# Two-layer diffusion backbone with a PEER expert layer, fp32: latent halves ahead of the context tokens in layer one, a pace of gathers worked out per run, and layer two's modulation moved into the context tokens' merge

## What is computed

```python
for l in range(DEPTH):
    mod_l = silu(c) @ w_mod + b_mod          # 6 x 1024, the same for all latent tokens
    mod_c = silu(c_ctx) @ w_mod + b_mod      # 6 x 1024, for all context tokens
    hl, hc = modulated rms_norm of xl, xc
    a_l = neighbourhood_attention(q_l, k_l, v_l, k_ctx, v_ctx, rpb)
    m_l = latent attention of xl over the keys of ctx and xl
    s_l = spatial_gating(...)
    xl_new = xl + mod_l[2] * branch_merge(a_l, s_l, m_l, ...)
    if not last:                              # context's own attention, merge: layer one alone
        xc = xc + mod_c[2] * branch_merge(a_c, s_c, m_c, ...)
    xl_new = xl_new + mod_l[5] * peer_ffn(h2, ...)
    if not last:
        xc = xc + mod_c[5] * peer_ffn(h2c, ...)
# peer_ffn: idx = the 16 best experts per head and token
#           act = gelu(sum(exp_u[idx] * h)); out = sum(gate * act * exp_v[idx])
```

## Time and profile before

| what | value |
|---|---|
| median of 3 runs | 5605.33 us (5599.78 to 5616.61) |
| profiled execution | 5615.22 us, span of its core 5613.4 us |
| TensorE busy | 4447.6 us (79%), mean granted clock 0.867 |
| VectorE busy | 3051.5 us (54%) |
| GpSimd busy | 2763.0 us (49%) |
| ScalarE busy | 1241.3 us (22%) |
| DMA | 1651.73 MB, 294 GB/s over the span |
| of it, gathers (software queue) | 1342.34 MB |

### The profile page before, as it was taken

How to read it: one execution, slowest core, us unless ns; L and a number is a source line. 1 busy time by engine, 2 the same in 40 slices (tenths; PEclk the granted TensorE clock), 3 DMA queues, 4 the chain that set the end, 5 groups by cost and what they waited for, 6 DMA issues and landing times.

```text
span 5613.4 us, 57357 instructions
## 1 busy us (share of the span) xinstructions
PE 4447.6 (79%) x19168; PEld 2455.9 (44%) x19168; DVE 3051.5 (54%) x8176; ACT 1241.3 (22%) x3643; POOL 2763.0 (49%) x2566
## 2 busy tenths in 40 slices
PE   7989798889997887997855558999788889655555
PEld 4467643433585344653411115558533455311111
DVE  0211767776217776556676542431677655777643
ACT  1321222333212321112211112540133211111111
POOL 0000466666304655666677770000366466777776
PEclk9889898888998888998977888999888999877778
DMA  5544799988747878999999992114688799999999
GB/s 189 189 153 142 282 367 340 335 311 331 253 137 279 324 286 304 379 398 358 356 390 369 394 389 83 55 39 154 221 310 318 278 366 399 391 391 391 362 403 353
DMA packets 464130, 1651.73 MB, mean 294 GB/s; under 512 B 51168, under 2 KB 57440, under 8 KB 463840
## 3 DMA queue, kind: packets, MB, share of 16 engines
q0 software_dynamic: 368640, 1342.34, 63.2%
q1 hardware_dynamic: 95200, 305.73, 15.2%
HBM read 1645.77 MB, written 2.10 MB: 294 GB/s over the span
## 4 chain that ended last, share of the span: by engine, by line
PE 50%; POOL 15%; DVE 13%; DMA 11%; issue 7%; ACT 3%; SPq 0%; DVEq 0%; POOLq 0%; ACTq 0%; PEldq 0%
PE banks L647 16%; PE banks L925 10%; DMA vb<-in_peer_v_dram,idx 8%; POOL vb L1446 8%; POOL ub L1435 7%; DVE ub L1386 5%; PE banks L736 4%; PE banks L663 3%; PE banks L773 3%; PE banks L835 3%; PE banks L812 2%; PE banks L758 2%; PE banks L823 1%; DMA ub<-in_peer_u_dram,idx 1%; PE banks L715 1%
## 5 line engine op out<-in xcount | busy, mean ns | idle before, releaser
L1435 POOL DMA_INDIRECT ub<-in_peer_u_dram,idx x1280 | 1424.1, 1113 | 2270.7 <-DVE idx L1374 1375.1
L925 PE MATMUL banks<-vb,dg 128*64 128x512 f32 x5120 | 1571.7, 741 | 695.7 <-DMA vb<-in_peer_v_dram,idx 626.4
L1386 DVE CUSTOM_DVE_ANT_0 ub<-ub,h2cur 128x1024 f32<-128x1024 f32 x1280 | 1529.6, 1223 | 611.1 <-DMA ub<-in_peer_u_dram,idx 485.9
L1446 POOL DMA_INDIRECT vb<-in_peer_v_dram,idx x1280 | 1338.3, 1046 | 561.0 <-issue 342.5
L925 PEld LDWEIGHTS banks<-vb,dg 128*64 128x64 f32 x5120 | 406.7, 160 | 1596.1 <-issue 1336.4
L647 PE MATMUL banks<-region,wring 128*128 128x256 f32 x3840 | 882.2, 390 | 35.8 <-ACT region L989 25.3
L647 PEld LDWEIGHTS banks<-region,wring 128*128 128x128 f32 x3840 | 738.7, 195 | 215.8 <-issue 104.9
L1135 ACT ACTIVATE dg<-consts,wgt 128x64 f32<-128x64 f32 x1280 | 358.4, 337 | 836.5 <-PE banks L925 425.3
L647 PE MATMUL banks<-h2T,wring 128*128 128x256 f32 x1280 | 316.9, 406 | 21.1 <-ACT h2T L989 21.1
L1329 DVE SCALAR_TENSOR_TENSOR region<-region,banks 128x256 f32<-128x256 f32 x120 | 50.5, 421 | 486.0 <-PE banks L647 485.9
L736 PE MATMUL banks<-region,wring 128*128 128x256 f32 (+1 forms) x1056 | 260.7, 404 | 48.0 <-ACT region L989 48.0
(11 more groups left out here) (146 smaller groups left out, 4004.9 us busy)
## 6 DMA issues: line engine op xcount, KB each, us to landing
wring<-w_gate_dram SPq DMA_DIRECT2D x120, 512.0 KB, 5.0
wring<-w_mod_dram SPq DMA_DIRECT2D x96, 512.0 KB, 4.6
wring<-w_pq_dram SPq DMA_DIRECT2D x80, 512.0 KB, 5.4
wring<-w_branch_dram SPq DMA_DIRECT2D x60, 512.0 KB, 3.6
wring<-w_out_dram SPq DMA_DIRECT2D x40, 512.0 KB, 4.7
ub<-in_peer_u_dram,idx POOLq DMA_INDIRECT x1280, 6.6
vb<-in_peer_v_dram,idx POOLq DMA_INDIRECT x1280, 6.6
region<-in_na_rpb_dram SPq DMA_DIRECT2D x64, 256.0 KB, 3.0
```

The source lines that it names most:

```text
L925: ins = nc.tensor.matmul(bank(ACC[a])[64 * g:64 * g + 64, :], dg[:, n % DG_RING, :], vb[:, n % V_RING, a * 512:(a + 1) * 512], start=first ...
L1386: nc.vector.tensor_tensor_reduce(out=ub[:, n % U_RING, :], in0=ub[:, n % U_RING, :], in1=h2cur[:, g, :], scale=1.0, scalar=0.0, op0=ALU.mu ...
L1435: pool.indirect_dma_start(ub[:, n % U_RING, :], None, u_rows, bass.IndirectOffsetOnAxis(ap=idx[:, u % IDX_RING, j:j + 1], axis=0)).then_in ...
L1446: pool.indirect_dma_start(vb[:, n % V_RING, :], None, v_rows, bass.IndirectOffsetOnAxis(ap=idx[:, u % IDX_RING, j:j + 1], axis=0)).then_in ...
```

## The change

1. **Order.** Layer one now computes context's keys and values (`"kc"`, without queries), then half A and half B's `kq_stage`, `na_stage` of both, and the rest of A and of B. Only then come context's own stages: `kq_stage` again, with queries (keys and values are computed a second time), attention, merge, query. `TILES` is reordered to A, B, context. Layer two begins with A and B, and takes context's keys last.
2. **Pace.** `schedule` is run twice. The first time it notes the cost at marks; between the third projection of one `query_stage` and that of the next lies one run. The second time each run gets its own cost per background step, so that some 120 steps fit: 4.3 within `query_stage`, and outside it 3.47 (half B, both layers), 4.04 to 4.84 (context) and 1.29 to 4.84 (layer two's `kq_stage`). By the numbers that the code computes, in order: 4.3, 3.4715, 4.3, 4.0435, 4.3, 1.2892, 4.3, 4.8393, 4.3, 3.4715.
3. **Modulation.** `modrow` has one buffer per layer, the first in `vb`, the second in `region`; `cS` and `cT` have tiles of their own (the index ring gives 22 to 21 for it). `modr` writes 2 rows of each group of 32, so ScalarE copies four pieces of 2x256 and not one of 128x256; and a chunk's `modt` stands ahead of the next chunk's `modr`. Layer two's 24 chunks are computed in context's `merge_stage`.

Counted from the list that each kernel builds (steps that have their dot products or their sums there):

| place | steps before (dots/sums) | after |
|---|---|---|
| layer one, ahead of the first query stage | 0 | 0 |
| layer one, first query stage | 13/2 (context) | 13/2 (half A) |
| B: mla, merge with the norm behind it, query (each layer) | 40, 46, 16 | 47, 56, 17 |
| layer one: kq A, kq B, na, mla A, merge A, query A | 18, 15, 41, 37, 4/15, 13/2 | none |
| context, layer one: kq, na, mla, merge with the norm, query | none | 18, 10, 18, 58, 16 |
| layer two: kq of context, kq A, kq B | 11, 17, 0 | 0, 57, 50 |
| forced, in layer two's start | 13, then 100/111 | 24/35 |
| layer two: na, mla A, merge A | 0 | 0 |
| forced, at the end | 141/152 | 123/134 |

The diff, cut to its core:

```diff
-U_RING, V_RING, IDX_RING, DG_RING = 6, 6, 22, 8
+U_RING, V_RING, IDX_RING, DG_RING = 6, 6, 21, 8
-BG_STEP = 4.2
+RUN, QUERY_STEP = 120, 4.3
...
-        TILES = [(0, 0), (0, 1), (0, 2), (0, 3), (0, 4), (0, 5), (1, 2), (1, 3), (1, 4), (1, 5)]
+        TILES = [(0, 2), (0, 3), (0, 4), (0, 5), (0, 0), (0, 1), (1, 2), (1, 3), (1, 4), (1, 5)]
...
         def emit(step, cost=0.0):
             plan.append(step)
-            owed[0] += cost
-            while owed[0] >= BG_STEP:
-                owed[0] -= BG_STEP
+            pace["cost"] += cost
+            if pace["steps"] is None or not pace["marks"]:
+                return
+            step_cost = pace["steps"][len(pace["marks"]) - 1]
+            pace["owed"] += cost
+            while pace["owed"] >= step_cost:
+                pace["owed"] -= step_cost
                 if not bg_step():
-                    owed[0] = 0.0
+                    pace["owed"] = 0.0
...
-                    emit(("modr", l, c), 1.2)
                     if c not in (0, 8):
                         emit(("modt", l, c - 1), 0.4)
+                    emit(("modr", l, c), 1.2)
...
+        def layer_tail(l, s):
+            mla_stage(l, s)
             fence()
+            if l == 0 and s == CTX_S:
+                mods.extend((1, c) for c in range(24))
+            merge_stage(l, s)
+            query_stage(l, s)
+            fence()
...
+            mods.extend((0, c) for c in range(8))
+            some_mods(8)
+            mods.extend((0, c) for c in range(8, 24))
+            kq_stage(0, CTX_S, False)
+            fence()
+            for l in range(LAYERS):
+                for s in (A_S, B_S):
+                    if l:
+                        until_tail(tile_no[(0, 2 * s + 1)])
+                    kq_stage(l, s, True)
+                    fence()
+                if l:
+                    mark()
+                    until_tail(tile_no[(0, 1)])
+                    mark()
+                    kq_stage(l, CTX_S, False)
+                    fence()
+                na_stage(l, (A_S, B_S))
                 fence()
+                layer_tail(l, A_S)
+                layer_tail(l, B_S)
+                if l == 0:
+                    kq_stage(0, CTX_S, True)
+                    fence()
+                    na_stage(0, (CTX_S,))
+                    fence()
+                    layer_tail(0, CTX_S)
+            while steps is not None and bg_step():
+                pass
+
+        schedule(None)
+        marks = pace["marks"] + [pace["cost"]]
+        steps = []
+        for n in range(0, len(marks) - 1, 2):
+            here, query_end, run_end = (marks + marks[-1:])[n:n + 3]
+            steps += [QUERY_STEP, (run_end - query_end) / (RUN - (query_end - here) / QUERY_STEP) + 1e-3]
+        schedule(steps)
...
-                    if cnt["mod"] >= 2:
-                        whole(act, mod_keys[-2])
-                    frees(nc.scalar.activation(modrow[:, cnt["mod"] % 2, :], bk[:, 0:256], ACT.Copy), key)
+                    if mod_keys:
+                        whole(act, mod_keys[-1])
+                    if n == 0:
+                        link(nc.scalar.activation(modrow_of[l], consts[:, 0:N], ACT.Copy, scale=0.0))
+                    for g in range(4):
+                        rows = slice(32 * g, 32 * g + 2)
+                        ins = nc.scalar.activation(modrow_of[l][rows, :], bk[rows, 0:256], ACT.Copy)
+                    frees(ins, key)
```

More of the change, by code:

```diff
@@ L251, in program @@
         plan = []
-        owed = [0.0]
-        bgs = dict(avail=0, front=0, d=0, g=0, a=0, rate=1)
-        TILES = [(0, 0), (0, 1), (0, 2), (0, 3), (0, 4), (0, 5), (1, 2), (1, 3), (1, 4), (1, 5)]
+        pace = dict(owed=0.0, cost=0.0, marks=[], steps=None)
+        bgs = {}
+        TILES = [(0, 2), (0, 3), (0, 4), (0, 5), (0, 0), (0, 1), (1, 2), (1, 3), (1, 4), (1, 5)]
+        tile_no = {lt: n for n, lt in enumerate(TILES)}
         def topk_step():
@@ L305, in emit, with mark @@
             plan.append(step)
-            owed[0] += cost
-            while owed[0] >= BG_STEP:
-                owed[0] -= BG_STEP
+            pace["cost"] += cost
[5 more added lines that the diff above has]
+                pace["owed"] -= step_cost
                 if not bg_step():
-                    owed[0] = 0.0
+                    pace["owed"] = 0.0
+        def mark():
+            pace["marks"].append(pace["cost"])
         def until_tail(tile):
-            while bgs["a"] < PAIRS * PH * (tile + 1):
+            while pace["steps"] is not None and bgs["a"] < PAIRS * PH * (tile + 1):
                 bg_step()
         def until_front(tile):
-            while bgs["d"] <= PAIRS * PH * tile:
+            while pace["steps"] is not None and bgs["d"] <= PAIRS * PH * tile:
                 bg_step()
-            while bgs["front"] < 7 * PH * (tile + 1):
+            while pace["steps"] is not None and bgs["front"] < 7 * PH * (tile + 1):
                 topk_step()
@@ L375, in kq_stage @@
             t0 = N * s
-            emit(("norm", l, s, "kq"), 6.0)
+            again = 1 if l == 0 and s == CTX_S and queries else 0
+            emit(("norm", l, s, "kq" if s or queries else "kc"), 6.0)
             emit(("h_wait", "kq"))
@@ L399, in values @@
                 for c in range(4):
-                    add_load((l, s, "v", c), w_v[l, c])
-                emit(("values", l, s), 14.0)
+                    add_load((l, s, "v", c, again), w_v[l, c])
+                emit(("values", l, s, again), 14.0)
                 some_mods(4)
@@ L522, in query_stage @@
         def query_stage(l, s):
-            assert not mods or l or s
+            assert not [m for m in mods if m[0] == l]
             if bgs["avail"]:
@@ L535, in query_stage @@
                     emit(("sc", l, s, cc - 1), 0.8)
+                if cc == 2:
+                    mark()
                 if cc and cc % 2 == 0:
@@ L570, in program, with schedule @@
-        while bg_step():
-            pass
+            mark()
+        def layer_tail(l, s):
+            mla_stage(l, s)
+            fence()
+            if l == 0 and s == CTX_S:
[3 more added lines that the diff above has]
+            fence()
+        def schedule(steps):
+            for a in (plan, loads, pace["marks"], bias_order, mods):
+                a.clear()
+            for a in (load_at, batches, units_of, bsb_no):
+                a.clear()
+            fences[0] = 0
+            pace.update(owed=0.0, cost=0.0, steps=steps)
+            bgs.update(avail=0, front=0, d=0, g=0, a=0, rate=1)
+            mods.extend((0, c) for c in range(8))
[10 more added lines that the diff above has]
+                if l:
+                    mark()
+                    until_tail(tile_no[(0, 1)])
+                    mark()
+                    kq_stage(l, CTX_S, False)
+                    fence()
+                na_stage(l, (A_S, B_S))
+                fence()
+                layer_tail(l, A_S)
[8 more added lines that the diff above has]
+                pass
@@ L600, in fence_wait @@
             eng.wait_ge(stage_end, 3 * n)
-        hT_of = {"kq": hT_kq, "mla": hT_mla, "mg": hT_mg, "n2": h2T}
-        tile_no = {lt: n for n, lt in enumerate(TILES)}
+        hT_of = {"kq": hT_kq, "kc": hT_kq, "mla": hT_mla, "mg": hT_mg, "n2": h2T}
         unit_list = [(l, t, h) for l, t in TILES for h in range(PH)]
@@ L651, in feature, with token_rows @@
                     last_by_bank(load, key)
-            def token_rows(l, s, what, src):
-                keys = [(l, s, what, t) for t in range(2)]
+            def token_rows(l, s, what, src, again=0):
+                keys = [(l, s, what, t, again) for t in range(2)]
                 bks = [fill(key) for key in keys]
                 for c in range(4):
-                    name = (l, s, what[0] if what == "vv" else "sv", c)
+                    name = (l, s, "v", c, again) if what == "vv" else (l, s, "sv", c)
                     w = weights(name)
@@ L789, in _ @@
                 elif op == "values":
-                    token_rows(step[1], step[2], "vv", h_src[0])
+                    token_rows(step[1], step[2], "vv", h_src[0], step[3])
                 elif op == "vm":
@@ L1009, in _ @@
                 elif op == "values":
-                    _, l, s = step
+                    _, l, s, again = step
                     dst = vnac if s == 0 else vnal
                     for t in range(2):
-                        key = (l, s, "vv", t)
+                        key = (l, s, "vv", t, again)
                         bk = whole(act, key)
```

71 lines of the change are left out of this document (20 added, 51 removed).

## The result

The changed kernel takes 5754.82 us (median of 4, 5745.99 to 5768.96) where the kernel before takes 5602.56 beside it: ratio 1.0272, 95% interval [1.0251, 1.0293]. It is slower by 2.7%; 0.4% faster was forecast. The profiled execution has a span of 5744.2 us against 5613.4, so 131 us are to be found.

The account below looks back on a forecast made before the run. No engine bounds throughout: TensorE in foreground alone, DMA in background alone, both nearly when woven. Eight stretches sum to 5582, 5586 with small extras, 5576 scaled to the median, plus 6: 5582 us against 5605.3; 8 in 10 from 5505 to 5665.

Parts of the forecast that it names:

- Merge with its norm: ten more at 3.5: Half B, layer one: ten added background steps at 3.5 us each take merge from 346.0 to 379 us.
- seven more at 2.6 to 3.0: Half B's mla, layer one: seven added background steps at 2.6 to 3.0 us each, 291.5 to 311 us.
- the rival of the full woven runs: Stretches mixing foreground and background are full, added steps cost 5.5 us: 5700 us; 0.30 together with the late modulation rival.
- its rival: Late modulation doesn't hide: TensorE waits 1.2 us for each of 48 loads, 58 us: 5640; 0.30 together with full runs.
- the forecast of 475 us: Context's merge, layer one: 193.5 alone, 85 for chunks and open waits, 56 steps at 3.5 us.
- 24 chunks at 3.2 us and open waits: Layer two's modulation in context's merge: the chunks at 3.2 us plus half of the waits open, 85 us.
- The bound of the forced stretch: Background without foreground: TensorE's sums wait for vb gathers, 2.10 MB a step at 410 GB/s, 5.12 us apart, called the floor.
- where I took 392: Layer two's kq A and B: DMA at 392 GB/s moves 107 steps and 30 loads, 240 MB, in 612 us.
- The start: Layer one up to the end of query A: 939 us against 656, 283 us more in which gathers stand still.
- the cheap steps: A step moved from a forced stretch into a woven one saves 2 to 3 us, nothing where DMA is full.
- the forced stretches: Background alone: 163 us behind layer two's kq stages for the last 35 sums, 709 us at the end, 18 steps fewer.
- layer two's kc: Context's keys and values in layer two's foreground: six items of ten, 78.3 - 20 = 58 us.

Follow-up runs that it names:

- e6: Changed kernel with peer_v gathers of half a row after the first six, half B of layer one at pace 4.2; 5749.93 us.
- e8: Changed kernel with only the first of a step's two peer_v gathers made, half B of layer one at pace 4.2; final forced stretch 589.3 us.
- e2b: Changed kernel with the modulation of before, all 48 chunks ahead of the first gather; 5672.47 us, ratio 1.0127 to the kernel before.
- e7: Changed kernel, products of gates, branches, output and query projections summing half their terms, layer one's B at pace 4.2; layer two's B 23 us shorter.
- e9: Changed kernel, modulation still late, with two modrow buffers per layer and each modt one chunk later; ratio 1.0118 to the kernel before, slower chip.
- e3b: Kernel before with the changed order alone, pace 4.2 and modulation of before; ratio 1.0097 to the kernel before.

## Why the forecast was wrong

- *The step that failed:* "Merge with its norm: ten more at 3.5" and "seven more at 2.6 to 3.0". I divided the difference between a stage alone and the same with 40 steps by 40, and used this mean as the price of the next step. The added ones cost 5.4 in B of both layers. From 81 to 102 steps they cost 3.2 on the mean, so the price was right for the paces it came from, and wrong for the next ones. This is the rival of the full woven runs; I had put the price at 5.5. It makes 79 of the 134 us by which the woven stretches were missed. The runs show in its place that GpSimd waits 184 us for slots in B at 102 steps and at 120 alike, so DMA shares of 0.87 to 0.93 leave no room to be filled; e6 to e8 add that neither the bytes nor TensorE's products set this price.
- *Late modulation:* its rival named waits for weights behind gathers, 58 us. They are there, 37.5 and 7.9 us, but they replace other waits in part, and the larger share of what the chunks cost context's stages is their own 50 us of products, which the forecast had. In context's merge the forecast of 475 us was met, 474.7, since I had priced 24 chunks at 3.2 us and open waits. That price was read from rows at half the clock: the earlier trace rows stand in 129.0 to 138.5 us, where the granted clock is 0.53 and the products of a chunk take 1.08 twice and 1.01, while in the merge they took 2.1 and in the start 1.7 in all. So the merge's total came out in part by luck, waits standing where I had products. What I did not see is what the price means beside 1.7 us a chunk in the start: the move itself loses, 85 us as measured in the whole kernel. The rest of context's miss is in mla (135 against 122), na (67 against 60) and kq (132 against 127), at the mean price again.
- *The bound of the forced stretch* was misread. "2.10 MB a step at 410 GB/s. That is the floor" is right as a number and wrong as a cause: GpSimd issues four gathers in 5.12 us, and with a quarter of the bytes gone the stretch was no shorter. DMA is at 0.99 there as well, so the two limits lie side by side, and the DMA share told only of one. Layer two's kq A and B took 5.98 us a step with their weights, at 374 GB/s, where I took 392. The 358 GB/s that the Trainium skill, page "DMA: Bandwidth & Descriptors", section "Where 436 GB/s comes from", gives as the bound would have made them 670 us; 374 passes it.
- *The start* was as forecast within 13 us: chunks 56.2 (55), the rest on rows of layer two. The higher cost of the order was in the sum from the beginning, 283 us, 296 measured. That it would be given back rested on the cheap steps.
- *Right:* the forced stretches (163 and 709; 171.7 and 708.9) and layer two's kc (58; 57.8).
- *What stays open:* how the 1.3% that order and pace cost together (e2b) splits on a fast chip. On slower ones the order alone has 1.0097 and 1.0143, and with the changed paces 1.0073. Also open is which of the mutual waits (GpSimd on VectorE's dot products, VectorE on TensorE's products, TensorE on the top-16) would have to go first in B's merge to shorten GpSimd's 184 us; e7, with 80 us less of TensorE's work, took only some 16 off them. Deeper rings were not tried.

## What to carry to other kernels

The mean price of background work in a woven stretch is not the price of the next piece: take it from two paces of the same stage, and expect it to rise to the price of running it alone. Look at what the issuer waits for: once an added piece no longer shortens those waits, it costs its full time. Pay attention to stretches in which the scarce issuer has nothing to do, and spread work evenly into them before making any stretch denser. Work that is moved from a quiet stretch into one full of gathers costs its own time there, makes an in-order engine wait for its loads, and holds up everything queued behind it. Take the price of a product from rows at the clock of the stretch into which it goes.

## What the runs showed of the hardware

- Indirect gathers of 128 rows followed one another on GpSimd at 1.24 to 1.28 us in the quickest rows, with rows of 4 KB (kernel before) and of 2 KB (e6) alike; over whole forced stretches the mean was 1.32, and 1.44 in e6, where some gathers of full rows took 1.44 to 1.76 us without the issue. 25% fewer bytes and about as many fewer packets brought nothing; 25% fewer gathers did.
- GpSimd made its gathers at 1.35 to 1.38 us each in B at every pace from 81 to 120 steps; what changed with the pace was only its waits for free slots, 240 us at 81 steps and 184 at 102 and at 120.
- Chips differ by 4% on this kernel (before: 5600 to 5605 us on three, 5836 to 5844 on two); the reason was not looked for. The foreground alone takes the same there (merge A 194.7 us in the changed kernel and in e9), the final forced stretch 866 us (e3b) against 808 (kernel before, as many gathers).
